# Nineteen taps of the last convolution chunk on VectorE, in three pauses, and the rest of the chunk behind the third pool projection

## The reference

```python
def conformer_conv_group(a, gate, w_dw, b_dw, ln_g, ln_b):
    u = a * jax.nn.sigmoid(gate)
    k = w_dw.astype(u.dtype)[:, None, :]
    v = lax.conv_general_dilated(u, k, window_strides=(1,), padding=[(CONV_WIDTH - 1, 0)],
        dimension_numbers=("NWC", "WIO", "NWC"), feature_group_count=C_CONV) + b_dw.astype(u.dtype)
    v = layernorm(v, ln_g, ln_b)
    return jax.nn.silu(v)
...
def second_block(...):
        z = xn @ w_in[l] + b_in[l]
        a = z[..., :C_CONV]
        gate = z[..., C_CONV:2 * C_CONV]
        p = z[..., 2 * C_CONV:]
        y_conv = conformer_conv_group(a, gate, w_dw[l], b_dw[l], ln_g[l], ln_b[l])
        y_pool = multiscale_pool_group(p, w_pool[l], s_pool[l])
        y = jnp.concatenate([y_conv, y_pool], axis=-1)
        h = h + y @ w_out[l]
```

## Time and profile before

| | us |
|---|---|
| median of 3 runs (lowest, highest) | 1761.96 (1761.55, 1762.08) |
| profiled execution, own time | 1761.59 |
| its span, first to last instruction | 1759.8 |
| TensorE busy | 1748.9 (99% of the span) |
| VectorE busy | 702.2 (40%) |
| ScalarE busy | 704.4 (40%) |
| GpSimd busy | 804.2 (46%) |

### The profile page before, as it was taken

One profiled execution on the slowest core, in us unless ns is written; L12 is line 12 of the kernel. 1 busy time (PEld: TensorE's weight loads), 2 busy tenths in 40 slices (PEclk: granted clock), 3 DMA queues, 4 the chain that ended last, 5 costly groups with the idle time before them and its releaser, 6 DMA issues.

```text
span 1759.8 us, 22952 instructions
## 1 busy us (share of the span) xinstructions
PE 1748.9 (99%) x8350; PEld 1423.2 (81%) x8350; DVE 702.2 (40%) x1111; ACT 704.4 (40%) x1110; POOL 804.2 (46%) x372
## 2 busy tenths in 40 slices
PE   9999999999999999999999999999999999999998
PEld 7888888888888777778888888888866888888887
DVE  5222240068777985236262222200786532222002
ACT  5222222256645477784252222221425432222224
POOL 2444444457666433335554444444543544444443
PEclk9999999999999999999999999999999999999999
DMA  5233232332333121113323222222352233322222
GB/s 175 97 99 100 98 96 96 97 124 87 109 108 120 64 74 60 49 38 100 100 92 98 100 96 95 96 95 95 102 144 64 93 98 98 99 97 95 96 95 84
DMA packets 50492, 168.20 MB, mean 96 GB/s; under 512 B 6264, under 2 KB 7032, under 8 KB 50304
## 3 DMA queue, kind: packets, MB, share of 16 engines
q1 hardware_dynamic: 47088, 161.34, 28.2%
q10 hardware_dynamic: 3344, 6.05, 1.2%
HBM read 161.84 MB, written 2.11 MB: 93 GB/s over the span
## 4 chain that ended last, share of the span: by engine, by line
PE 93%; DVE 5%; ACT 1%; issue 1%; DMA 0%; POOL 0%; SPq 0%; DVEq 0%; ACTq 0%; POOLq 0%
PE bank L581 27%; PE bank L582 26%; PE bank L583 26%; PE bank L799 7%; PE bank L845 2%; DVE bank L1853 1%; PE bank L873 1%; PE bank L864 1%; PE bank L969 1%; DVE token_factor L1489 0%; DVE top_keys L1709 0%; DMA residual<-x_t 0%; DVE top L1708 0%; PE bank L662 0%; PE bank L722 0%
## 5 line engine op out<-in xcount | busy, mean ns | idle before, releaser
L496 POOL TENSOR_TENSOR weights_low<-raw_weights,weights_high 128x1024 fp32r<-128x1024 f32 x292 | 705.6, 2419 | 861.7 <-ACT weights_high L1077 833.6
L581 PE MATMUL bank<-input_high,weights_high 128*128 128x512 f32 x1424 | 559.0, 393 | 2.8 <-DVE input_low L1772 1.3
L582 PE MATMUL bank<-input_high,weights_low 128*128 128x512 f32 x1424 | 554.3, 389 | 0.0
L583 PE MATMUL bank<-input_low,weights_high 128*128 128x512 f32 x1424 | 554.3, 389 | 0.0
L1077 ACT CAST weights_high<-raw_weights 128x1024 fp32r<-128x1024 f32 x294 | 306.4, 1045 | 304.5 <-DMA raw_weights<-weights 283.9
L581 PEld LDWEIGHTS bank<-input_high,weights_high 128*128 128x128 f32 x1424 | 267.3, 188 | 64.6 <-issue 6.6
L582 PEld LDWEIGHTS bank<-input_high,weights_low 128*128 128x128 f32 x1424 | 267.4, 188 | 55.9 <-issue 1.4
L583 PEld LDWEIGHTS bank<-input_low,weights_high 128*128 128x128 f32 x1424 | 267.4, 188 | 55.9
L582 PE MATMUL bank<-hidden_high,weights_low 128*128 (+1 forms) x530 | 205.7, 388 | 0.0
L583 PE MATMUL bank<-hidden_low,weights_high 128*128 (+1 forms) x530 | 205.7, 388 | 0.0
L581 PE MATMUL bank<-hidden_high,weights_high 128*128 (+1 forms) x530 | 205.7, 388 | 0.0
(11 more groups left out here) (252 smaller groups left out, 1831.0 us busy)
## 6 DMA issues: line engine op xcount, KB each, us to landing
raw_weights<-weights SPq DMA_DIRECT2D x294, 512.0 KB, 3.3
out<-out_rows SPq DMA_DIRECT2D x8, 256.0 KB, 2.8
residual<-x_t SPq DMA_DIRECT2D x6, 256.0 KB, 5.9
glu_stacked<-glu_padded SPq DMA_DIRECT2D x24, 64.0 KB, 2.1
glu_stacked<-glu_padded ACTq DMA_DIRECT2D x24, 64.0 KB, 2.1
mem_in<-mem_t ACTq DMA_DIRECT2D x1, 1024.0 KB, 4.7
tile<-forget_sums ACTq DMA_DIRECT2D x4, 256.0 KB, 3.4
raw_weights<-weights SPq DMA_DIRECT2D x3, 256.0 KB, 5.7
```

Source lines behind the costliest of these rows:

```text
L496: pool.tensor_tensor(wl[:, u % RING, :], raw[:, u % RING, :], wh[:, u % RING, :].bitcast(F32), ALU.subtract).then_inc(low_done, 1)
L581: pe.matmul(out, wh[:, u % RING, w], rh, start=start, stop=False)
L582: pe.matmul(out, wl[:, u % RING, w], rh, start=False, stop=False)
L583: return pe.matmul(out, wh[:, u % RING, w], rl, start=False, stop=stop)
```

## The change

Chunk 3 is shared between the engines. VectorE does its first 19 taps: three ahead of the first pool window, seven behind it, nine behind the second. TensorE's share of the chunk begins at group 5, which leaves 12 products of 32, and they stand behind projection 10 (the third pool projection) where they stood behind projection 9. ScalarE's copy of the bank for chunk 3 is gone; VectorE adds the bank to its own sum (`merge_last`), right behind its take of projection 10, and that add sets `conv_done` to 2. The table of tap weights grows by the 31 columns of chunk 3.

```diff
-CONV_AFTER = {6: 1, 8: 2, 9: 3}
-FIRST_GROUP = {1: 2, 2: 0, 3: 0}
-DVE_TAPS = {0: TAPS, 1: STACK * FIRST_GROUP[1] - 1}
+CONV_AFTER = {6: 1, 8: 2, 10: 3}
+FIRST_GROUP = {1: 2, 2: 0, 3: 5}
+DVE_TAPS = {0: TAPS, 1: STACK * FIRST_GROUP[1] - 1, 3: STACK * FIRST_GROUP[3] - 1}
+TAP_COLS = {0: 0, 1: 1, 3: 2}
+BEFORE_WINDOW, BEHIND_WINDOW = 3, 7
...
-        tap_sums, conv_bank, maps = {0: bank[2], 1: bank[4]}, bank[6], [bank[5], bank[4]]
+        tap_sums, conv_bank, maps = {0: bank[2], 1: bank[4], 3: bank[2]}, bank[6], [bank[5], bank[4]]
...
-                if CONV_AFTER.get(j, 1) != 1:
-                    take_conv(CONV_AFTER[j])
+                if CONV_AFTER.get(j) == 2:
+                    take_conv(2)
...
-                        w, src, total = v("w_dw_2", c * TAPS + k), glu[:, c, k:k + S], tap_sums[c][:, :]
+                        w, src, total = v("w_dw_2", TAP_COLS[c] * TAPS + k), glu[:, c, k:k + S], tap_sums[c][:, :]
...
+            def merge_last():
+
+                dve.wait_ge(sem("taps_summed"), 3)
+                dve.wait_ge(sem("taps_gathered"), 3)
+                dve.wait_ge(sem("conv_done"), 1)
+                dve.tensor_tensor(conv[:, 3, :], conv[:, 3, :], conv_bank[:, :], ALU.add).then_inc(sem("conv_done"), 1)
...
                 if kind == "p":
+                    if c == 0:
+                        for _ in range(BEFORE_WINDOW):
+                            next(conv_taps)
+                    if c == 2:
+                        merge_last()
                     windows(c)
+                    if c == 0:
+                        for _ in range(BEHIND_WINDOW):
+                            next(conv_taps)
+                    if c == 1:
+                        for _ in conv_taps:
+                            pass
```

More of the change, by code:

```diff
@@ L98 @@
                   ("dsa_k_norm", 1), ("mem_q_norm", 1), ("mem_k_norm", 1), ("b_forget", HEADS), ("b_in_2", 12),
-                  ("w_dw_2", 2 * TAPS), ("w_taps_2", CONV_BLOCKS * TAP_GROUPS), ("b_dw_2", 4), ("ln_g_2", 4), ("ln_b_2", 4), ("s_pool_2", 4),
+                  ("w_dw_2", 3 * TAPS), ("w_taps_2", CONV_BLOCKS * TAP_GROUPS), ("b_dw_2", 4), ("ln_g_2", 4), ("ln_b_2", 4), ("s_pool_2", 4),
                   ("inv_freq", 1), ("pool_inv", len(WINDOWS) * PADW)):
@@ L1893, in _ @@
                 if j:
-                    total = sum(DVE_TAPS.values())
+                    total = DVE_TAPS[0] + DVE_TAPS[1]
                     for _ in range(min(STEP_TAPS[kind], total - done)):
@@ L2025, in vectors @@
     taps = np.concatenate([np.zeros((1, BW), np.float32), a["w_dw_2"][0]])
-    put("w_dw_2", a["w_dw_2"][0].reshape(TAPS, 4, P)[:, :2].transpose(2, 1, 0).reshape(P, 2 * TAPS))
+    put("w_dw_2", a["w_dw_2"][0].reshape(TAPS, 4, P)[:, list(TAP_COLS)].transpose(2, 1, 0).reshape(P, 3 * TAPS))
     taps = taps[:, P:]
```

## The result

The changed kernel takes **1765.33 us**, median of 13 runs (1764.77 to 1766.52), against 1762.1 of the kernel before in as many runs beside it: a ratio of 1.0019, 95% interval 1.0012 to 1.0026. It is slower by 3.2 us. The profiled execution took 1764.99 us, with a span of 1763.2 against 1759.8.

A forecast was written before the change was run, and what follows sets the result against it. TensorE was taken as the bound, with 93% of the chain of waits. A later VectorE take and layer-norm wait (together +2.0, 0.2 swallowed by the clock) left 1.8 + 2.4 = +4.2 us: 1766.1 us, range 1761.0 to 1767.5.

The forecast's parts named there:

- The likeliest case: VectorE held by GpSimd in window 2, and TensorE's clock falls in the resulting idle: 1766.1 us, chance 0.45.
- the clock's term: TensorE idles some 6 us ahead of the output projection, then runs slowly as at the program's start: +2.4 us.
- Products saved: 20 of chunk 3's 32 tap products leave TensorE, so everything behind them could come 4.4 us earlier.
- The pauses for the taps: VectorE's 19 taps: three and seven hidden in pauses, nine end about 1333.95, so projection 10's take starts about 1333.9.
- The holds: Three GpSimd instructions hold window 2's two adds and narrow multiplication on VectorE, the third bounded by 0 and 2.2 us.
- The take of projection 11: VectorE's take, ahead of the output projection, is done at 1344.3, 2.1 us later; TensorE's second product comes +1.8 us.
- The layer norm's squares: Squares' sum behind the output projection's second product: TensorE waits some 0.2 us more, swallowed by the clock's 2.4 us.
- That idleness brings the low clock: TensorE's idle of some 6 us ahead of the output projection returns the array to 1.2 GHz.
- Held with the clock at its full level: Rival: window 2 on VectorE is held but TensorE's clock stays: +2.0 us, 1763.9 us, chance 0.27.
- Not held: Rival: GpSimd's three instructions slip behind window 2, so VectorE isn't held: 1758.5 us, or 1757.6, chance 0.09.
- One hold fewer: Rival: window 2's narrow multiplication gets in ahead of GpSimd's second split: about 1762, up to 1763 us, chance 0.11.
- the two largest chances: Forecast outcomes for the whole kernel: within 0.2% of before, chance 0.52; slower, from 1765.5 us, chance 0.40.

The follow-up runs named there:

- filled pause: Changed kernel plus six extra 128x512 products, result unread, in TensorE's queue ahead of the wait: 1763.56 us, ratio 1.001 against the kernel before.
- splits beside the taps: Changed kernel, nineteen taps, GpSimd's two weight splits started behind window 1 and one ScalarE cast a projection earlier: 1759.48 us, ratio 0.9986 against the kernel before.
- fifteen taps: Changed kernel with 15 taps on VectorE and 16 products on TensorE, GpSimd's order unchanged: 1760.47 us; with the two splits beside the taps 1758.40 us.
- the version without a hold in window 2: Nineteen taps, splits beside them, third convolution sum moved from GpSimd to VectorE behind the merge: 1758.96 us, ratio 0.9983 against the kernel before.

## Why the prediction was right, step by step

The forecast was 1766.1 us in a range of 1761.0 to 1767.5; the median is 1765.33. The likeliest case is the one that came. How near the number came is chance in part: the median is the highest run of the lower group, and two more runs in the upper one would have made it 1766.0, all but the forecast, though the clock's term was too large.

- **Products saved (4.4 us).** TensorE stands at the layer norm's sum at 1337.65 instead of 1341.88: 4.2 us. Right.
- **The pauses for the taps.** The seven taps end in time: the take of projection 9 starts at 1322.39 (forecast 1322.25). The ninth of the last taps ends at 1334.01 (1333.95), and the take of projection 10 starts at 1333.93. Right; in the version with the splits beside them the taps cost the same.
- **The holds.** Forecast ends were 1337.1, 1339.95 and 1342.2; the rows give 1337.12, 1339.88 and 1342.10. The third was the one that no row of before showed, bounded by 0 and 2.2 us: a multiplication of 16 columns took 2.19 us. The Trainium skill ("SBUF — State Buffer", section "SBUF: two separate sides") has the shared ports as a lock held for a whole instruction, without an exception for narrow ones. This case's traces agree: held instructions of 16 columns took 2.19, 2.22, 2.25 and 2.29 us.
- **The take of projection 11** is done at 1344.10 (forecast 1344.3), the second product starts at 1344.75 (1344.8): +1.78 us, as the sum had it. Here two errors cancel: the take was 0.2 us early, and the step from the first product to the second took 0.59 us at the low clock, where the sum had 0.34 at the full one.
- **The layer norm's squares (+0.2 us, swallowed by the clock).** Right both ways: behind the pause it adds 0.02 us, and with the clock at its full level the distance from second product to squares is 7.21 us (filled pause) against 7.03, so 0.18.
- **The clock (2.4 us): the mis-sized term.** The mechanism came as said, a fall in the middle of the program after an idle of TensorE, but it cost 1.6 to 1.8 us (filled pause), in the trace 1.59 behind the second product and 0.25 ahead of it. I took the price from the program's opening, where the products start at the low pace. Here the pause begins at 1344.16 - 5.49 = 1338.67 and the clock falls at 1341.4, so 2.7 us of the low stretch lie over idle time; from 1344.16 to 1348.2 TensorE works 4.1 us in it, at half pace some 2 us. That opening was no firm price, either: the same 14 records take 4.85 us in one execution of the changed kernel and 6.04 in another.
- **That idleness brings the low clock** had no row in the middle of a program before. Now the granted clock stands at 0.50 from 1342 to 1348, which is the level of 1.2 GHz. The Trainium skill ("TensorE: Matmul & The Clock Gate", section "Part 1: The HAM clock gate (the "warmup" mystery)") says that an idle array returns to 1.2 GHz; the trace agrees. Pauses of 1.45 and 1.63 us (splits beside the taps; fifteen taps) left the clock at 1.00.
- **The rivals.** Held with the clock at its full level was priced at 1763.9 us; the filled pause gives 1763.56. Not held was priced at 1758.5; the version without a hold in window 2, with one more add on VectorE, gives 1758.96. One hold fewer did not come, since the narrow multiplication waited; letting the splits start earlier only moved holds to window 1.

The interval of the ratio, 1.0012 to 1.0026, lies across the 0.2% that the prediction took as its bound, where slower and no difference meet; these had the two largest chances.

## What to carry to other kernels

A queue that is released by a new event moves everything behind it: ask not only when the released instruction runs but which of the other engine's instructions it then runs beside. Where two engines hold each other, put the one's work beside those instructions of the other that don't take part (here GpSimd's splits beside taps that accumulate in PSUM): the same nineteen taps go from 1765.3 to 1759.5 us by that order, with one cast a step earlier. And offload as much as the receiving engine can finish before the first engine arrives, no more: of the two counts tried in that order, fifteen taps gave 3.45 us against the kernel before and nineteen 2.4.

## What the runs showed of the hardware

- A narrow instruction with two SBUF inputs is held like a wide one: 16 columns, 0.17 us alone, took 2.19 to 2.29 us when a GpSimd split of 128x1024 was running, and two such in a row were each held, by one split each.
- VectorE's taps (one tensor in SBUF, the running sum in PSUM) are not held at all: 6.29 us for eight with GpSimd busy or idle. The kind of instruction is not what matters: one of the taps' kind with both tensors in SBUF took 2.38 instead of 0.74 us beside a split. GpSimd is held, too: two splits take 4.72 us beside the taps and 5.42 to 5.52 us beside an add and a narrow multiplication.
- The granted clock fell to 0.50 in pauses of TensorE of 5.5 and 4.4 us and just after one of 2.9 us, and not in pauses of 1.34, 1.45 and 1.63 us. What it costs is the work that is left in the low stretch, not the stretch: 1.6 to 1.8 us of time for a low stretch from 1341.4 to 1348.2.
- The clock can also fall at the very end, while small products run: the last 32 transposes took 3.69 us in two executions and 5.36 us in a third of the same kernel, and 0.7 us of the time came from there. Differences of under 1 us between kernels with that end can come from it, so they should rest on medians of several runs.
